# Handing over between two stages of a decoder step: the first gate weights and h loaded in the stage before, the sample's rows handed on in SBUF

## The chip, the cores and the metric

The kernel runs on one core of one Trainium2 chip, as one launch. The metric is the time of one execution on the device in microseconds (us), median of a few runs. fp32 throughout; matrix products are made exact enough by splitting each operand into a high and a low part (three products instead of one).

## The reference, cut to what matters

One layer of a decoder on a prompt of 2048 rows and on 32 sample rows (8 sequences x 4 positions), D_MODEL 1024:

```python
h = rms_norm(x, norm1_g) * (1 + scale1) + shift1
u, v_a, q, k, v_b, gates = jnp.split(h @ w_in, PROJ_SPLITS, axis=-1)
out_a = chunk_spatial_gate(gelu(u), layer_norm(gelu(v_a)), w_s, b_s)      # mixer A, 512 wide
out_b = attention(rope(q), rope(k), v_b)                                   # mixer B, 512 wide
g_a, g_b = split(sigmoid(gates))
merged = g_a * (out_a @ w_pa) + g_b * (out_b @ w_pb)
x = x + gate1 * (merged @ w_o)
# then: adaLN norm, top-2 of 32 experts, second residual, final norm
```

The sample rows go through the same weights; their attention also reads a cache of 128 keys and values for each of the 8 sequences.

## The kernel before, in words

The program has two Blocks, one behind the other. In a Block each of the five engines has its own list of instructions; engines meet only at semaphores, and at the end of a Block all five meet at a barrier, GpSimd clears the semaphores of the stage, and they meet again (`tools`, lines 111 to 128).

**The first Block, `sweep_mixers`**, goes over 16 tiles of 128 prompt rows and, as a 17th tile (index S), the 32 sample rows. It has the weights of both mixers in SBUF (`w_mix_hi`, `w_mix_lo`), computes h of a tile, turns it and stores its high and low parts as `hT_split` in DRAM; the results of mixers A and B go, turned and split, to `oT_split`. For the sample tile, ScalarE rounds a high part (L450, L507, L579), VectorE makes the low part (L594, L658, L814), and SyncE stores them (L315, L328, L381). The last steps of the Block are the sample's attention over the cache: TensorE L991 and L992, VectorE L810, ScalarE L579, VectorE L814, SyncE L381. SyncE then waits until every store has landed.

**The second Block, `finish`**, starts with `gate_a`: for each of 17 tiles, h times the gate columns of `w_in` (8 slices of 128 rows), out_a times `w_pa` (4 slices), out_b times `w_pb` (4 slices). SyncE loads the 16 slices (L1066, L1079; 512 KB each) into `w_gate_raw` and `w_out_raw`, and between them the sample's h and results (L1042, L1047, forms of 32 columns) and those of the first prompt tile. ScalarE rounds slice k (L1125), VectorE makes its low part in place of the raw one (L1160) once TensorE has used the raw slice for the sample rows (L1248). VectorE adds the sample's high and low parts up again into `sample_T` (L1164, L1169). In `first_tiles` TensorE takes the sample rows one slice ahead of the first prompt tile: sample(0), sample(1), slice 0, sample(2), slice 1 and so on. Then come two products with `w_ada` (L1281) and tiles 2 to 16 in a loop, each of which waits for its loads. Order on SyncE is the order in the code: the 16 slices, `w_ada` twice, then the loads of tile 2.

The same raw places are filled a second time by `gate_b`. Up to here slices k and k+8 share a semaphore (`raw_in[k % 8]`).

Of the kernel before, what the change touches and what calls it, by code (L numbers as in the profile page):

```python
# [92 lines left out]
def program(nc, a, outs):  # L93
    stack = ExitStack()
    with stack:
# [18 lines left out]
        }  # L114
        sweep_mixers(nc, a, s, kept, outs)
# [41 lines left out]
def sweep_mixers(nc, a, s, kept, outs):  # L157
# [3 lines left out]
    with ExitStack() as ctx:  # L161
        sb, sem = tools(nc, ctx)
        ps = banks(nc, ctx, "mix")
        with nc.sbuf_tensor("w_mix_raw", [P, KD, MIX_COLS], F32) as w_raw:
            pass
# [5 lines left out]
        wa = (w_hi, w_lo)  # L171
        x = sb("x_rows", [P, D])
        hT = [sb(f"hT_{n}", [P, KD, P], F32R) for n in ("hi", "lo")]
        mod = sb("mod_prompt", [P, 2, D])
        mod_s = sb("mod_sample", [MS, 2, D])
# [12 lines left out]
        obT_f = sb("out_b_T_sample", [P, 4, MS])[:, :, :]  # L188
# [17 lines left out]
        sq = sb("squares", [P, D])  # L206
# [20 lines left out]
        smp_turned, smp_scored, smp_dve, smp_max, smp_out = [sem(f"sample_{n}") for n in ("turned", "pe", "dve", "max", "out")]  # L227
# [32 lines left out]
        def _(sp):  # L260
# [61 lines left out]
            def rows_a(i, m):  # L322
                sp.wait_ge(oaT_lo, i + 1)
                dst = s["oT"][bass.ds(i, 1), 0, :, :] if not isinstance(i, int) else s["oT"][i:i + 1, 0, :, :]
                if m == P:
                    sp.dma_start(dst.rearrange("o p c -> p (o c)"), oaT[:, :, :].rearrange("p n c -> p (n c)").bitcast(F32)).then_inc(stored_oa, 16)
                else:
                    sp.dma_start(dst.rearrange("o p (c m) -> p (o c) m", m=P)[:, :, 0:m],  # L328
                                 oaT[:, :, :].rearrange("p n (k m) -> p (n k) m", m=P)[:, :, 0:m].bitcast(F32)).then_inc(stored_oa, 16)
# [16 lines left out]
            rows_a(0, P)  # L346
            with sp.Fori(1, NT - 2) as i:
                angles(i + 1, P)
                rows_b(i - 1)
                ahead(i + 2)  # L350
                stores(i + 1, P)
                rows_a(i, P)
# [7 lines left out]
            rows_a(NT - 2, P)  # L360
# [6 lines left out]
            stores(S, MS)  # L367
            rows_a(NT - 1, P)
# [69 lines left out]
        def _(act):  # L438
# [63 lines left out]
            def out_a(i, m, first):  # L502
# [3 lines left out]
                view = lambda t: t.rearrange("p (k m) -> p k m", m=P)[:, :, 0:m]  # L506
                nc.scalar.copy(view(oaT[:, 0, :]), view(ps[2][:, :])).then_inc(oaT_hi, 1)  # L507
# [8 lines left out]
            def tile(i, first=False, m_next=P):  # L516
# [15 lines left out]
                out_a(i, P, first)  # L532
# [38 lines left out]
            out_a(S, MS, False)  # L571
# [5 lines left out]
            act.wait_ge(smp_out, 1)  # L577
            act.wait_ge(stored_ob, 16 * NT)
            nc.scalar.copy(obT[:, 0, :].rearrange("p (k m) -> p k m", m=P)[:, :, 0:MS], obT_f).then_inc(obT_hi, 1)  # L579

        @block.vector
        def _(dve):
# [72 lines left out]
            def low_a(i, m):  # L655
                dve.wait_ge(oaT_hi, i + 1)
                view = lambda t: t.rearrange("p (k m) -> p k m", m=P)[:, :, 0:m]
                nc.vector.tensor_tensor(view(oaT[:, 1, :]), view(ps[2][:, :]), view(oaT[:, 0, :]).bitcast(F32),  # L658
                                        ALU.subtract).then_inc(oaT_lo, 1)
# [46 lines left out]
            def tile(i, mask_i, first=False, m_next=P, g_next=mod):  # L706
# [12 lines left out]
                low_a(i, P)  # L719
# [52 lines left out]
            low_b(NT - 1)  # L772

# [10 lines left out]
            low_a(S, MS)  # L784
# [23 lines left out]
            for g in range(NKV):  # L808
                src = ps[6][g * HD:(g + 1) * HD, 0:DEC_B * HQ].rearrange("p (b g c t) -> p g c b t", b=DEC_B, g=NKV, c=NC)[:, g]
# [191 lines left out]
def gate_a(nc, a, s, kept, sem, ps, weights, shared):  # L1001

    with ExitStack() as ctx:
# [5 lines left out]
        hb = sb("h_parts", [P, 2, 2 * D], F32R)  # L1009
# [10 lines left out]
        sample_h, sample_o, summed = sem("ga_sample_h"), sem("ga_sample_o"), sem("ga_sample_summed")  # L1020
        first_h, tile_in = sem("ga_first_h"), (sem("ga_tile_in0"), sem("ga_tile_in1"))
# [9 lines left out]
        landed = lambda k: 16 * (k // 8 + 1) + (16 if k >= KD + 4 else 0)  # L1031

        def slices():
            for k in range(KD):
                yield a["w_in"][0, k * P:(k + 1) * P, GATE_A:GATE_A + D]
            for k in range(4):
                yield a["w_pa"][0, k * P:(k + 1) * P, :]

        def on_sync(sp):
            def load_h(tile, par, m, done=None):  # L1040
# [1457 lines left out]
```

## Time and profile before

| | |
|---|---|
| time, median of 3 runs | 2024.82 us (2024.26 to 2030.19) |
| the profiled execution | 2026.46 us |
| its span, first to last instruction | 2024.8 us |
| TensorE busy in the span | 1896.6 us (94%) |
| TensorE's granted clock, mean | 0.960 of 2.4 GHz |
| DMA, mean | 188 GB/s |

In the rows below, TensorE appears twice: PE is the matmul, PEld the load of its stationary operand, which overlaps. DVE is VectorE, ACT ScalarE, POOL GpSimd; SPq is SyncE's queue, which issues DMAs. A name before `<-` is written, the names behind it are read; `L1248` is a line of the kernel. A bracket at the end of a row says how long the engine had been idle and what ended that. Times on the left are microseconds from the span's start, and where busy time is given it is not yet the time that the chain needs: matmuls are pipelined and overlap one another.

### The profile page before, as it was taken

The page shows a single profiled execution, that of the slowest core. Times are in us where ns is not written, and L with a number is a line of the kernel's source. Part 1 is how long each engine was busy: PE and PEld are TensorE (multiplying, and loading weights), DVE is VectorE, ACT ScalarE, POOL GpSimd, SP SyncE. Part 2 cuts the span into 40 slices and gives each one's busy share as a digit, 9 for nine tenths or more (in the row PEclk, how much of TensorE's full clock was granted, in tenths as well). Part 3 has the DMA queues.
Part 4 walks back from the last instruction along what each step waited for, and adds up shares of the span by engine and source line. Part 5 has one row for each costly group of instructions (what it writes and reads, how often), then busy time and mean ns, then how long its engine had stood idle before and what let it go on. Part 6 is the DMA issues. An engine that isn't in the chain of part 4 may idle for free.

```text
span 2024.8 us, 29311 instructions
## 1 busy us (share of the span) xinstructions
PE 1896.6 (94%) x9169; PEld 1427.9 (71%) x9170; DVE 1082.2 (53%) x1901; ACT 752.1 (37%) x1318; POOL 328.6 (16%) x337
## 2 busy tenths in 40 slices
PE   6999999999699999998999999992999999999966
PEld 2778877877367777776888888872667777776622
DVE  4777777777330000014455555555666666666647
ACT  3445554444221001013111111112566666666612
POOL 0111101110000000001011111101233333333411
PEclk7999999999699999999999999995999999999978
DMA  9212222122485554448444444437497464889686
GB/s 376 108 75 86 106 105 97 74 96 95 130 302 181 197 201 166 170 153 325 157 145 145 145 145 145 145 132 264 152 349 273 141 213 142 314 286 364 218 317 283
DMA packets 184473, 380.60 MB, mean 188 GB/s; under 512 B 41116, under 2 KB 112972, under 8 KB 177232
## 3 DMA queue, kind: packets, MB, share of 16 engines
q1 hardware_dynamic: 145824, 319.10, 44.1%
q0 software_dynamic: 20848, 52.32, 6.8%
q10 hardware_dynamic: 17760, 8.67, 1.5%
q8 instruction: 22, 0.36, 0.1%
q14 instruction: 19, 0.16, 0.0%
HBM read 295.16 MB, written 104.26 MB: 197 GB/s over the span
## 4 chain that ended last, share of the span: by engine, by line
PE 63%; DMA 4%; DVE 3%; issue 1%; SPq 1%; ACT 1%; ACTq 0%; POOL 0%; DVEq 0%; POOLq 0%
PE fin L152 16%; PE fin L154 15%; PE fin L153 15%; PE fin L2353 9%; PE fin L2322 2%; PE fin L1771 2%; PE fin L1807 1%; DMA w_gate_raw<-in_w_in 1%; DMA mixer_parts<-oT_split 1%; PE fin L1281 1%; DVE expert_gate_up L2298 1%; PE fin L2393 1%; DVE expert_gate_up L2302 1%; DMA w_out_raw<-in_w_o 1%; DVE expert_down L2291 1%
## 5 line engine op out<-in xcount | busy, mean ns | idle before, releaser
L2250 DVE TENSOR_TENSOR gate_up_lo<-expert_gate_up,gate_up_hi 128x2048 fp32r<-128x2048 f32 x102 | 233.6, 2292 | 149.0 <-ACT gate_up_hi L2155 145.6
L2155 ACT CAST gate_up_hi<-expert_gate_up 128x2048 fp32r x102 | 194.6, 1909 | 87.5 <-issue 87.5
L152 PE MATMUL mix<-w_mix_hi,hT_hi 128*128 128x512 f32 (+3 forms) x544 | 203.1, 373 | 3.8 <-DVE hT_lo L594 2.5
L153 PE MATMUL mix<-w_mix_hi,hT_lo 128*128 128x512 f32 (+3 forms) x544 | 198.7, 365 | 0.0
L154 PE MATMUL mix<-w_mix_lo,hT_hi 128*128 128x512 f32 (+3 forms) x544 | 198.2, 364 | 0.0
L2353 PE MATMUL fin<-expert_down,hidden_T 128*128 x400 | 182.6, 600 | 4.8 <-ACT hidden_T L2163 4.2
L1189 DVE SCALAR_TENSOR_TENSOR ma_rows<-tanh_rows,fin 128x512 f32<-128x512 f32 x32 | 20.6, 684 | 311.3 <-PE fin L154 160.9
L152 PE MATMUL fin<-gate_up_hi,gathered_T_hi 128*128 128x512 f32 x400 | 161.7, 404 | 4.2 <-DVE gathered_T_lo L2241 4.2
L154 PE MATMUL fin<-gate_up_lo,gathered_T_hi 128*128 128x512 f32 x400 | 158.1, 395 | 0.0
L153 PE MATMUL fin<-gate_up_hi,gathered_T_lo 128*128 128x512 f32 x400 | 157.6, 394 | 0.0
L2085 POOL DMA_INDIRECT gathered<-h_rows,row_tokens x52 | 130.0, 2501 | 43.8 <-PE fin L2322 17.9
L2353 PEld LDWEIGHTS fin<-expert_down,hidden_T 128*128 128x128 f32 x400 | 73.0, 193 | 78.5 <-issue 78.5
L152 PEld LDWEIGHTS mix<-w_mix_hi,hT_hi 128*128 128x128 f32 (+1 forms) x544 | 100.6, 185 | 37.2 <-issue 20.3
L154 PEld LDWEIGHTS mix<-w_mix_lo,hT_hi 128*128 128x128 f32 (+1 forms) x544 | 100.5, 185 | 19.1
L2091 POOL DMA_INDIRECT weighted_rows<-y_block,row_records x50 | 63.4, 1268 | 302.7 <-ACT y_block L2171 290.8
L153 PEld LDWEIGHTS mix<-w_mix_hi,hT_lo 128*128 128x128 f32 (+1 forms) x544 | 100.7, 185 | 16.2
L152 PE MATMUL fin<-w_gate_hi,h_parts_b 128*128 128x512 f32 x256 | 102.6, 401 | 6.0 <-issue 4.8
L152 PE MATMUL fin<-w_out_hi,merged_T_hi 128*128 128x512 f32 x256 | 102.3, 400 | 2.5 <-issue 2.5
L152 PE MATMUL fin<-w_gate_hi,h_parts 128*128 128x512 f32 x256 | 102.8, 402 | 1.0 <-DMA mixer_parts<-oT_split 1.0
L153 PE MATMUL fin<-w_out_hi,merged_T_lo 128*128 128x512 f32 x256 | 100.8, 394 | 0.0
L154 PE MATMUL fin<-w_out_lo,merged_T_hi 128*128 128x512 f32 x256 | 100.6, 393 | 0.0
L152 PE MATMUL fin<-w_out_hi,mixer_parts 128*128 128x512 f32 x256 | 100.5, 393 | 0.0
(343 smaller groups left out, 3769.1 us busy)
## 6 DMA issues: line engine op xcount, KB each, us to landing
expert_gate_up<-in_w_gate SPq DMA_DIRECT2D x32, 1024.0 KB
expert_gate_up<-in_w_up SPq DMA_DIRECT2D x32, 1024.0 KB
expert_down<-in_w_down SPq DMA_DIRECT2D x32, 1024.0 KB
h_parts<-hT_split SPq DMA_DIRECT2D x16, 1024.0 KB, 5.2
mixer_parts<-oT_split SPq DMA_DIRECT2D x32, 512.0 KB, 8.2
w_ada_part<-in_w_ada SPq DMA_DIRECT2D x16, 1024.0 KB, 10.6
h_parts_b<-hT_split SPq DMA_DIRECT2D x16, 1024.0 KB, 4.8
expert_down<-weighted_rows SPq DMA_DIRECT2D x12, 1024.0 KB, 7.9
```

Source lines behind the costliest of these rows:

```text
L152: nc_mm(out, left[0], right[0], start=first, stop=False)
L153: nc_mm(out, left[1], right[0], start=False, stop=False)
L154: return nc_mm(out, left[0], right[1], start=False, stop=last)
L1189: last = nc.vector.scalar_tensor_tensor(out=ma[:, par, at], in0=tg[:, at], scalar=1.0, in1=ps[2 + n][:, :], op0=ALU.add, op1=ALU.mult)
L1281: done = nc.tensor.matmul(ps[6 + half][32 * j:32 * j + R, :], c_now[half][:, :], wc[half][:, j, :], start=first, stop=last, tile_position= ...
L1771: last = nc.tensor.transpose(ps[bank + k // 4][:, (k % 4) * P:(k % 4 + 1) * P], src[:, k * P:(k + 1) * P], ident[:, :])
L2085: pool.indirect_dma_start(out=xg[:, slot % 2, :], out_offset=None, in_=s["h2"], in_offset=bass.IndirectOffsetOnAxis(ap=idx[:, slot, 0:1].b ...
L2091: pool.indirect_dma_start(out=s["y2"], out_offset=bass.IndirectOffsetOnAxis(ap=rec[:, slot, 0:1].bitcast(U32), axis=0), in_=y[:, half(slot ...
L2155: nc.scalar.copy(wg[par][0][:, n * HG:(n + 1) * HG], ring[:, bass.ds(slot * GU + n * HG, HG)]).then_inc(w_hi, 1)
L2250: nc.vector.tensor_tensor(wg[par][1][:, at], ring[:, bass.ds(slot * GU + n * HG, HG)], wg[par][0][:, at].bitcast(F32), ALU.subtract).then_ ...
L2322: last = nc.tensor.transpose(ps[k // 4][:, (k % 4) * P:(k % 4 + 1) * P], xg[:, par, k * P:(k + 1) * P], ident[:, :])
L2353: last = nc.tensor.matmul(ps[5 + n][:, :], hT[par][:, k, :], downs[:, bass.ds(at, 512)], start=(k == 0), stop=(k == 1))
```

## The change: what it does

1. The places of the gate weights, of `sample_T` and of `h_parts` are laid out before the first Block (`gate_places`), over the mixers' weights and, for h, over `hT`; their load semaphores live for the whole program (`kept`), one for each of the 16 slices. The small lists of `finish` move out of their way, and so do x, the squares and two modulation rows of the mixers. As `kept` things now have semaphores of the program's own scope, one more clearing with its barriers stands at the end of the program.
2. At the end of its work in the mixers' Block, once TensorE has used the mixers' weights for the last time (`u_done` of tile S) and all prompt h is stored, SyncE issues all 16 weight slices and the h of the first prompt tile. It doesn't wait for them there.
3. The sample's h and results are no longer stored and loaded. VectorE adds h's two parts into `sample_T` directly, and copies out_a and out_b from PSUM into it.
4. `gate_a` thus starts with weights that are there or on their way; its SyncE list begins with the first tile's results.

```diff
@@ sweep_mixers, SyncE @@
             rows_b(NT - 2)
-            stores(S, MS)
-            rows_a(NT - 1, P)
+            rows_a(NT - 1)
             rows_b(NT - 1)
...
             sp.wait_ge(ln_ready, S + 1)
             sp.dma_start(chunk_v[0].rearrange("b t w -> (b t) w"), v[0:MS, :]).then_inc(stored_kv, 16)
-            rows_a(S, MS)
-            sp.wait_ge(obT_lo, S + 1)
-            sp.dma_start(s["oT"][S, 1].rearrange("p (c m) -> p c m", m=P)[:, :, 0:MS],
-                         obT[:, :, :].rearrange("p n (k m) -> p (n k) m", m=P)[:, :, 0:MS].bitcast(F32)).then_inc(stored_ob, 16)
+            sp.wait_ge(u_done, S + 1)
+            sp.wait_ge(stored_h, 32 * NT)
+            for k, src in enumerate(gate_slices(a)):
+                sp.dma_start(gate_raw(k), src).then_inc(kept["raw_in"][k], 16)
+                if k == 1:
+                    sp.wait_ge(smp_kept, 1)
+                    sp.dma_start(first_h[:, 1, :].bitcast(F32), s["hT"][0]).then_inc(kept["first_h"], 16)
+            for c in range(NC):
+                for g in range(NKV):
+                    k, h = KD + 4 + c, g * NC + c
+                    sp.dma_start(gate_raw(k)[g * HD:(g + 1) * HD], a["w_pb"][0, h * HD:(h + 1) * HD, :]).then_inc(kept["raw_in"][k], 16)
             sp.wait_ge(stored_kv, 80)
-            sp.wait_ge(stored_h, 32 * (NT + 1))
-            sp.wait_ge(stored_oa, 16 * (NT + 1))
-            sp.wait_ge(stored_ob, 16 * (NT + 1))
+            sp.wait_ge(stored_oa, 16 * NT)
+            sp.wait_ge(stored_ob, 16 * NT)
@@ ScalarE @@
             gelu_u(S, MS, False)
-            out_a(S, MS, False)
...
-            act.wait_ge(smp_out, 1)
-            act.wait_ge(stored_ob, 16 * NT)
-            nc.scalar.copy(obT[:, 0, :].rearrange("p (k m) -> p k m", m=P)[:, :, 0:MS], obT_f).then_inc(obT_hi, 1)
@@ VectorE @@
             low_b(NT - 1)
+            nc.vector.tensor_tensor(sample_T[:, 0:KD, :], hT[0][:, :, 0:MS].bitcast(F32), hT[1][:, :, 0:MS].bitcast(F32), ALU.add).then_inc(smp_kept, 1)
...
-            low_a(S, MS)
+            dve.wait_ge(oa_turned, S + 1)
+            nc.vector.tensor_copy(sample_T[:, KD:KD + 4, :], ps[2][:, :].rearrange("p (k m) -> p k m", m=P)[:, :, 0:MS]).then_inc(smp_kept, 1)
...
-                last = nc.vector.tensor_copy(obT_f[g * HD:(g + 1) * HD, :, :].rearrange("p c (b t) -> p c b t", t=DEC_T), src)
-            last.then_inc(smp_out, 1)
-            dve.wait_ge(obT_hi, S + 1)
-            view = lambda t: t.rearrange("p (k m) -> p k m", m=P)[:, :, 0:MS]
-            nc.vector.tensor_tensor(view(obT[:, 1, :]), obT_f, view(obT[:, 0, :]).bitcast(F32), ALU.subtract).then_inc(obT_lo, 1)
+                nc.vector.tensor_copy(sample_T[rows, KD + 4:, :].rearrange("p c (b t) -> p c b t", t=DEC_T), src).then_inc(smp_kept, 1)
@@ gate_a, SyncE @@
-            for k, src in enumerate(slices()):
-                if k >= 8:
-                    sp.wait_ge(raw_hi, k - 7)
-                sp.dma_start(raw(k), src).then_inc(raw_in[k % 8], 16)
-                if k == 0:
-                    load_h(NT, 0, MS, sample_h)
-                    load_h(0, 1, P, first_h)
-                if k == 4:
-                    load_o(NT, 0, MS, sample_o)
-                if k == KD:
-                    load_o(0, 1, P)
...
+            load_o(0, 1)
             load_ada(0, 0)
             load_ada(0, 1)
             load(2, 0)
@@ gate_a, VectorE @@
-            dve.wait_ge(sample_h, 16)
-            nc.vector.tensor_tensor(sample_T[:, 0:KD, :], parts[:, 0:KD, :], parts[:, KD:, :], ALU.add).then_inc(summed, 1)
...
+            low(range(KD + 4))
@@ gate_a, TensorE, sample(k) @@
-                if k in (0, KD):
-                    pe.wait_ge(summed, 3 if k else 1)
-                pe.wait_ge(raw_in[k % 8], landed(k))
+                pe.wait_ge(raw_in[k], landed(k))
```

How SyncE's list changes around the border of the two Blocks. Before, from the store of the sample's v to the last load of tile 2 (the two branches are the border):

```order
L378 DMA out<-v_rows 32x512
L328 DMA oT_split<-out_a_T 1024x1x32
L381 DMA oT_split<-out_b_T 1024x1x32
L161 UNCONDITIONAL_BRANCH
L2443 UNCONDITIONAL_BRANCH
L1066 DMA w_gate_raw<-in_w_in 128x1024
L1042 DMA h_parts<-hT_split 128x16x32
L1042 DMA h_parts<-hT_split 128x2048
L1066 DMA w_gate_raw<-in_w_in 128x1024 x4
L1047 DMA mixer_parts<-oT_split 128x8x32 x2
L1066 DMA w_gate_raw<-in_w_in 128x1024 x3
L1066 DMA w_out_raw<-in_w_pa 128x1024
```

and the same stretch now, up to the results of tile 2:

```order
L383 DMA out<-v_rows 32x512
L387 DMA w_gate_raw<-in_w_in 128x1024 x2
L390 DMA h_parts<-hT_split 128x2048
L387 DMA w_gate_raw<-in_w_in 128x1024 x6
L387 DMA w_out_raw<-in_w_pa 128x1024 x4
L394 DMA w_out_raw<-in_w_pb 64x1024 x8
L168 UNCONDITIONAL_BRANCH
L2435 UNCONDITIONAL_BRANCH
L1044 DMA mixer_parts<-oT_split 128x1024 x2
L1056 DMA w_ada_part<-in_w_ada 128x4x512 x2
L1039 DMA h_parts<-hT_split 128x2048
L1044 DMA mixer_parts<-oT_split 128x1024 x2
```

Twenty weight loads and one of h stand ahead of the border instead of behind it, and the four small sample transfers in each direction are gone. VectorE's list at the end of the first Block, before:

```order
L805 COPY probs_T<-mix 128x256
L806 COPY probs_T<-mix 4x256
L810 COPY out_b_T_sample<-mix 64x128 x2
L814 TENSOR_TENSOR out_b_T<-out_b_T_sample,out_b_T 128x4x32
L161 UNCONDITIONAL_BRANCH
L2461 UNCONDITIONAL_BRANCH
L1164 TENSOR_TENSOR sample_T<-h_parts 128x256
L1160 TENSOR_TENSOR w_gate_lo<-w_gate_raw,w_gate_hi 128x1024 x4
```

and now:

```order
L811 COPY probs_T<-mix 128x256
L812 COPY probs_T<-mix 4x256
L817 COPY sample_T<-mix 64x128 x2
L168 UNCONDITIONAL_BRANCH
L2453 UNCONDITIONAL_BRANCH
L1139 TENSOR_TENSOR w_gate_lo<-w_gate_raw,w_gate_hi 128x1024 x8
```

The copy from PSUM is the last step of the Block now, and the first low part the first step of the next.

## Rows read from the trace of the kernel before

**Rows 1.** The page: busy time, share of the span and instructions of TensorE.

```profile
PE 1896.6 (94%) x9169; PEld 1427.9 (71%) x9170; DVE 1082.2 (53%) x1901; ACT 752.1 (37%) x1318; POOL 328.6 (16%) x337
```

**Rows 2.** Waits, 505 to 600 us: who waited for whom, total us, times, longest.

```profile
PE fin L1248 <- DVE sample_T L1164: 10.8, 1, 10.8
...
DVE sample_T L1164 <- DMA h_parts<-hT_split: 9.1, 1, 9.1
...
PE fin L1248 <- DMA w_gate_raw<-in_w_in: 3.2, 1, 3.2
```

**Rows 3.** Windows: stretch, its length, busy us by engine, granted clock, DMA share, GB/s.

```profile
524.00:533.60 9.60, 9.09 (x32) 7.99 (x32) 0.42 (x3) 0.00 (x0) 0.00 (x0) 0.50 0.00 0
...
549.60:553.40 3.80, 3.80 (x18) 2.03 (x14) 1.23 (x1) 3.14 (x3) 0.00 (x0) 0.50 1.13 308
553.40:584.80 31.40, 31.40 (x201) 17.83 (x199) 19.38 (x21) 13.21 (x15) 1.41 (x2) 1.00 1.02 357
...
587.70:610.70 23.00, 22.99 (x105) 18.10 (x105) 1.37 (x3) 1.92 (x4) 0.53 (x1) 1.00 0.61 228
```

**Rows 4.** Timeline, 533.4 to 540 us, all engines: start, us, engine, line, operation.

```profile
533.56 0.59 DVE L810 COPY out_b_T_sample<-mix 64x128 f32<-64x128 f32 x2 [9.18 <-PE mix L992]
...
534.52 0.29 DVE L814 TENSOR_TENSOR out_b_T<-out_b_T_sample,out_b_T 128x128 fp32r<-128x128 f32 x1 [0.36 <-ACT out_b_T L579]
534.84 0.55 SPq L381 DMA_DIRECT2D oT_split<-out_b_T  x1
538.84 0.37 SPq L1066 DMA_DIRECT2D w_gate_raw<-in_w_in  x1
```

**Rows 5.** Lines 161, 127, 128 (barriers, clearing): ns min/median/max, first and last start.

```profile
L161 SPq DRAIN x1: 13/13/13, 537.5 to 537.5; - x1
...
L127 POOLq EVENT_SEMAPHORE_RANGE_CLEAR  x2: 568/676/783, 538.0 to 2023.8; - x2
...
L128 SPq DRAIN  x2: 7/7/7, 537.8 to 2023.5; - x2
...
L128 SPq EVENT_SEMAPHORE  x2: 17/17/17, 538.8 to 2024.8; - x2
```

**Rows 6.** Timeline of TensorE, 533 to 588 us.

```profile
544.37 1.08 PE L1248 MATMUL fin<-w_gate_raw,sample_T 128*32 128x256 f32 x8 [10.85 <-DVE sample_T L1164]
...
549.62 0.80 PE L152 MATMUL fin<-w_gate_hi,h_parts 128*128 128x512 f32 x1
...
553.49 0.54 PE L152 MATMUL fin<-w_gate_hi,h_parts 128*128 128x512 f32 x1
...
584.78 1.91 PE L1281 MATMUL fin<-w_ada_part,c_now 128*9 128x512 f32 x16
587.71 0.49 PE L152 MATMUL fin<-w_gate_hi,h_parts 128*128 128x512 f32 x1 [1.02 <-DMA mixer_parts<-oT_split]
```

**Rows 7.** Timeline of SyncE's queue, which issues DMAs: three stretches.

```profile
2.07 3.68 SPq L266 DMA_DIRECT2D w_ada_slices<-in_w_ada  x7
...
9.06 13.65 SPq L275 DMA_DIRECT2D w_mix_raw<-in_w_in  x8
...
516.69 0.32 SPq L378 DMA_DIRECT2D out<-v_rows  x1
...
556.03 4.99 SPq L1079 DMA_DIRECT2D w_out_raw<-in_w_pb  x8
```

**Rows 8.** Groups of ScalarE and VectorE, 538 to 588 us: busy us, mean ns.

```profile
L1160 DVE TENSOR_TENSOR w_gate_lo<-w_gate_raw,w_gate_hi 128x1024 fp32r<-128x1024 f32 x8 | 9.8, 1226 | 11.3 <-PE fin L1248 10.3 <-ACT w_out_hi L1125 0.9
...
L1125 ACT CAST w_gate_hi<-w_gate_raw 128x1024 fp32r<-128x1024 f32 x8 | 8.4, 1050 | 16.0 <-DMA w_gate_raw<-in_w_in 16.0
```

**Rows 9.** Timeline of VectorE, 512 to 522 us.

```profile
515.19 1.29 DVE L782 COPY x_rows<-mix 128x512 f32<-128x512 f32 x2 [1.62 <-PE mix L821]
```

**Rows 10.** DMA queues, 516 to 520, then 538.8 to 587.7 us: packets, MB, share.

```profile
q8 instruction: 1, 0.02, 1.5%
...
q8 instruction: 2, 0.03, 0.2%
```

More of the change, by code:

```diff
@@ L114, in program @@
         }
+        sb, sem = tools(nc, stack)
+        kept["small"] = sb("small", [P, 48])
+        kept["half"] = sb("minus_half_row", [P, 1])
+        kept["rms"] = sb("rms_c", [P, 4, 4])
+        kept["lists"] = list_tables(sb)
+        kept["raw_in"], kept["first_h"] = [sem(f"g_raw_in{n}") for n in range(2 * KD)], sem("ga_first_h")
+        kept["gates"] = gate_places(nc)
         sweep_mixers(nc, a, s, kept, outs)
@@ L163, in sweep_mixers @@
         ps = banks(nc, ctx, "mix")
+        raws, _, sample_T, first_h = kept["gates"]
+        gate_raw = lambda k: raws[k // KD][:, k % KD, :]
         with nc.sbuf_tensor("w_mix_raw", [P, KD, MIX_COLS], F32) as w_raw:
@@ L500, in gelu_u, with out_a @@
                 nc.scalar.activation(u[0:m, :], ps[2][0:m, :], ACT.Gelu_apprx_tanh).then_inc(u_gelu, 1)
-            def out_a(i, m, first):
+            def out_a(i, first):
                 act.wait_ge(oa_turned, i + 1)
@@ L531, in tile @@
                 high(i + 1, m_next)
-                out_a(i, P, first)
+                out_a(i, first)
                 softmax(i)
@@ L1123, in high @@
                 for k in ks:
-                    act.wait_ge(raw_in[k % 8], landed(k))
+                    act.wait_ge(raw_in[k], landed(k))
                     nc.scalar.copy(w(0, k), raw(k)).then_inc(raw_hi, 1)
@@ L1160, in low @@
                     nc.vector.tensor_tensor(w(1, k), raw(k), w(0, k).bitcast(F32), ALU.subtract).then_inc(raw_lo, 1)
-            dve.wait_ge(sample_h, 16)
-            parts = view(hb[:, 0, :].bitcast(F32), MS, 16)
-            nc.vector.tensor_tensor(sample_T[:, 0:KD, :], parts[:, 0:KD, :], parts[:, KD:, :], ALU.add).then_inc(summed, 1)
-            low(range(4))
-            dve.wait_ge(sample_o, 32)
-            for n in range(2):
-                parts = view(ob[:, 0, n, :].bitcast(F32), MS, 8)
-                nc.vector.tensor_tensor(sample_T[:, KD + 4 * n:KD + 4 * n + 4, :], parts[:, 0:4, :], parts[:, 4:, :], ALU.add).then_inc(summed, 1)
-            low(range(4, KD + 4))
+            low(range(KD + 4))
             dve.wait_ge(tanhed, 1)
@@ L1742, in sample @@
             def sample(bank, lhs, k0, k, done):
-                pe.wait_ge(raw_in[(k0 + k) % 8], landed(k0 + k))
+                pe.wait_ge(raw_in[k0 + k], landed(k0 + k))
                 for j in range(4):
@@ L1869, in load_down, with list_tables @@
     sp.dma_start(ww, a["w_down"][0, bass.ds(e, 1), :, :].rearrange("o (k p) d -> p (o k) d", p=P)).then_inc(done, 16)
[L1872 removed]
+def list_tables(sb):
     ni = sb("blocks_i", [P, NE], I32)
@@ L1882, in list_blocks, with gate_places, gate_slices @@
     rest = sb("pairs_after_first", [1, 1], I32)
+    return ni, n, zero, ends, ends_i, m, f, lists, rest
+def gate_places(nc):
+    with ExitStack() as ctx:
+        split, raws = [], []
+        for m in ("gate", "out"):
+            with nc.sbuf_tensor(f"w_{m}_raw", [P, KD, D], F32) as w_raw:
+                raws.append(w_raw)
+            lo, hi = [ctx.enter_context(nc.sbuf_tensor(f"w_{m}_{n}", [P, KD, D], F32R)) for n in ("lo", "hi")]
+            split.append((hi, lo))
+        sample_T = ctx.enter_context(nc.sbuf_tensor("sample_T", [P, 2 * KD, MS], F32))
+        h_parts = ctx.enter_context(nc.sbuf_tensor("h_parts", [P, 2, 2 * D], F32R))
+        return raws, split, sample_T, h_parts
+def gate_slices(a):
+    for k in range(KD):
+        yield a["w_in"][0, k * P:(k + 1) * P, GATE_A:GATE_A + D]
+    for k in range(4):
+        yield a["w_pa"][0, k * P:(k + 1) * P, :]
+def list_blocks(nc, kept, sem, ps, small, ready):
+    ni, n, zero, ends, ends_i, m, f, lists, rest = kept["lists"]
     step_done, listed, moved = sem("l_step"), sem("l_listed"), sem("l_moved")
```

102 lines of the change are left out of this document (39 added, 63 removed).

## The prediction

> **What bounds the kernel now.** I read the busy shares first. TensorE is busy for 94% of the span [rows 1], so the place to look is where it is not. The waits of the stretch around the border of the two Blocks come next: TensorE stands 10.8 us until the sample's h is in SBUF, whose addition had itself waited 9.1 us for the DMA that brings it back from DRAM, then 3.2 us for the second weight slice [rows 2], and 1.02 us for the results of tile 2 [rows 6]. The windows show what follows: from 553.40 to 584.80 TensorE is busy for all of 31.40 us at clock 1.00, and tile 2, 587.70 to 610.70, takes 23.00 us of which 22.99 are busy [rows 3]. So once `gate_a` is under way it is bound by TensorE, and what is saved ahead of its first slice should pass to the end.
>
> **The hand-over (parts 2 and 3 of the change).** Before, the Block's last steps are: copy L810, 533.56 to 534.15; ScalarE L579; VectorE L814 to 534.81; store L381, issued at 534.84; the first DMA of the next Block at 538.84 [rows 4]. SyncE reaches the barrier at 537.5, when that store has landed, and goes on at 538.8 after the clearing [rows 5]. So barrier, clearing and barrier take 1.3 us, and the DMA follows at once. Now the copy is the last step, since SyncE waits only for stores issued by 516.69 and earlier [rows 7]. The Block's work ends at 534.15, the next begins at 534.15 + 1.3 = 535.5, that is 3.3 us earlier.
>
> **The additions on VectorE.** The sum of h's parts into `sample_T` is one instruction more, priced like the removed L1164, some 0.4 us. VectorE has 1.62 us of idle time ahead of L782 right behind it [rows 9], so it costs nothing; if that cover were missing, it would cost 0.4. The copy of out_a replaces L658 and ScalarE's part goes: nothing on the path either, since the chain behind it goes over TensorE's scores.
>
> **SyncE's 21 issues ahead of the border.** They start at 516.69 + 0.32, about 517.1 (`u_done` and the prompt stores are older). Seven loads of 1 MB are issued in 3.68 us, 0.53 each, and eight of `w_pb` in 4.99, 0.62 each, part of it waiting [rows 7]. 13 x 0.53 + 8 x 0.62 = 11.9, so SyncE is through by 529, 5 us before VectorE. Could its queue fill up, so that it holds the Block? In the trace it does at 9.06, where eight loads of 0.9 MB take 13.65 us [rows 7], but by then over 8 MB had been issued in 7 us. Here 9.4 MB in all are issued over 12 us; at 357 GB/s, the rate of the busy stretch [rows 3], 4 MB of it have landed by then, so 5 MB are in flight. I take no delay; the upper end is in a rival below.
>
> **The first slice.** Slice 0 and 1 and h were issued first and have landed by the border (2 MB at 357 GB/s is 6 us, hence by 525). What stands ahead of TensorE's slice 0 is then the high part, 1.05 us, and the low part, 1.23 us [rows 8], each with about 0.1 us of signalling. The sample groups sample(0) and sample(1) run beside them, 1.08 us each at the low clock [rows 6]. 535.5 + 0.1 + 1.05 + 0.1 + 1.23 + 0.1 = 538.1. Before, slice 0 starts at 549.62 [rows 6]. **Term 1: 549.62 - 538.1 = 11.5 us earlier.** Behind it ScalarE (1.05 per slice) and VectorE (1.23) are faster than TensorE, which takes (584.78 - 553.49) / 15 = 2.1 per slice [rows 6], so neither becomes the bound.
>
> **The clock.** The granted clock is 0.50 already while TensorE works on the small products of the sample's attention, 524.00 to 533.60, stays there over the idle time, and is still 0.50 for 549.60 to 553.40, when slice 0 runs; it is 1.00 from 553.40 [rows 3]. That is 1.2 and then 2.4 GHz. TensorE's dense work began only 1 us before slice 0. Now two sample groups, 2.1 us, run nearly straight into slice 0, so between 0 and 2.1 us of the slow stretch fall on them instead, and each such microsecond is worth half. A value in the middle: **term 2: 0.5 us gained** (0 to 1.05). The bound below nothing: if the short gap between sample(1) and slice 0 delays the rise by as long as the slow stretch before, 3.8 us, it costs 1.9.
>
> **The loads of tile 2.** Before, all transfers from 538.84 up to tile 2's amount to 14.7 MB, and TensorE waits 1.02 us for the last of them [rows 6]. Now 9.4 MB start at 517.1 and are in by 543.5 at 357 GB/s; 5.2 MB more (tile 1's results, two of `w_ada`, tile 2) are queued from 535.5 and are in by 558. TensorE gets to tile 2 at 538.1 + (584.78 - 549.62) - 0.5 + 1.9 = 574.7, so 16 us later than needed. **Term 3: 1.0 us gained.**
>
> **The clearing at the program's end.** Another clearing and barrier: the one at the end of the span goes from 2023.5 to 2024.8, of which the clearing is 0.57 to 0.78 us; that at the border goes from 537.8 to 538.8 [rows 5]. **Term 4: 1.2 us lost** (0 to 1.3).
>
> **The other layout.** New addresses and sixteen load semaphores instead of eight change no duration that the trace shows; later stages stand as they were. Nothing, either way.
>
> **Sum.** 11.5 + 0.5 + 1.0 - 1.2 = 11.8 us. The profiled execution took 2026.46 us, 1.64 above the median of the runs shown; I take the gain off each alike: 2014.7 for an execution like it, 2013.0 for the median. With the bounds of the terms, 11.5 + 1.05 + 1.0 - 0 = 13.6 and 11.5 - 1.9 + 1.0 - 1.3 = 9.3, this case alone gives 2011.2 to 2015.5.
>
> **Rival 1: the engines get going later than SyncE.** That engines start 0.1 us behind the barrier is seen only of SyncE [rows 4, 5]. The others waited for data there: the first high part starts 3.9 us behind the barrier. A start-up of up to 3.9 us was hidden and would show now: gain 7.9, time 2016.9. For it: nothing in the trace excludes it. Against: a fetch of instructions lies at 516 to 520, ahead of the border [rows 10], so that the code behind it may be at hand.
>
> **Rival 2: the barrier waits for the loads, or the transfers bind.** SyncE drains at the border for 13 ns [rows 5], but with all DMAs landed; no row shows a drain with loads in flight. Did it wait, the Block would end at 543.5, slice 0 start at 543.5 + 1.3 + 2.6 = 547.4: gain 2.2 + 0.5 + 1.0 - 1.2 = 2.5, time 2022.3. A full queue that holds SyncE gives something between this and the forecast. Against: the list of waits ahead of the border has no load in it.
>
> **Rival 3, slower: the loads hold up the tail of the first Block.** The mixers' tail fetches code at 516 to 520 [rows 10], just when 9.4 MB are put on the same 16 DMA engines. If that fetch is served behind them it comes at 543.5, and an engine that needs it stands: the remaining 16 us of the tail (518 to 534) then end at 559.5, slice 0 starts at 559.5 + 1.3 + 2.6 = 563.4, 13.8 us later than before: 2024.82 + 13.8 - 1.5 + 1.2 = 2038.3. It makes the change a loss once the fetch is delayed by more than about 12 us. Against it: two such fetches fall into 538.8 to 587.7 [rows 10], where the DMA engines are full, and TensorE is busy there for 31.40 of 31.40 us once it has begun [rows 3].
> The Trainium skill ("DMA: Bandwidth & Descriptors", section "Queues, rings and completion order") says that a DMA engine goes round its queues packet by packet, by which a fetch is delayed by a packet, not by 9 MB, and this rival would cost nothing; the full stretch above agrees. The same page, under "Back-pressure in remote DMA", says that writes stalled at a full SBUF port stall that engine's other queues too; it speaks of transfers between cores, and no row here shows such a stall. By it some of this rival's price would be due.
>
> **How the numbers follow.** What a measurement can tell from no change is about 0.3%, 6.1 us: faster is below 2018.7, slower above 2030.9. The forecast has 0.74, rival 1 0.12, rival 2 0.07, rival 3 0.04, others 0.03. Faster: the forecast and rival 1 and a part of the rest, 0.87; the same: rival 2, 0.08; slower 0.05. The time is the forecast's, 2013.0. The range takes the forecast's bounds with the scatter of a median, 2009.5 below, and rival 1 above with some of what lies between it and rival 2: 2018.5.
>
> **What would show it.** Right: the first DMA of the second Block near 535.5; slice 0 near 538; TensorE with no wait for a DMA from there to tile 2, which starts near 575 instead of 587.71; the span's end 12 us earlier with a second clearing of about 1.2 us in it. SyncE's 21 issues over by 529. Term 2 shows in the length of the stretch at clock 0.50 behind 538. Wrong: a first high part much later than the first DMA (rival 1), a border near 544 (rival 2), TensorE's attention products later than 524.4 (rival 3), or waits for transfers that come back in the loop of tiles.

## The result, and the profile after

| | before | changed |
|---|---|---|
| median of 4 runs | 2025.74 us (2024.26 to 2030.19) | 2013.88 us (2013.14 to 2014.41) |
| ratio | | 0.9939, 95% interval 0.9927 to 0.9952 |
| span of the profiled execution | 2024.8 us | 2012.8 us |

The changed kernel is about 12 us faster, 0.6%; by the interval the gain lies between 9.7 and 14.8 us. Forecast were 2013.0 us for the median and a gain of 11.8. Two runs lay far above all others of their kernel (10828 us in e3_late_first_h, 6324 us in g2_lead_again) and are left out of the medians and ratios below.

SyncE's queue in the changed kernel (start, us, queue, line, what it issues), from the first early load to the loads of tile 2; it answers to [rows 7] and to the last two of [rows 4]:

```profile
517.15 0.86 SPq L387 DMA_DIRECT2D w_gate_raw<-in_w_in  x2
518.06 0.43 SPq L390 DMA_DIRECT2D h_parts<-hT_split  x1
518.53 3.14 SPq L387 DMA_DIRECT2D w_gate_raw<-in_w_in  x6
521.71 2.59 SPq L387 DMA_DIRECT2D w_out_raw<-in_w_pa  x4
524.35 6.63 SPq L394 DMA_DIRECT2D w_out_raw<-in_w_pb  x8
535.69 0.81 SPq L1044 DMA_DIRECT2D mixer_parts<-oT_split  x2
...
539.73 6.85 SPq L1039 DMA_DIRECT2D h_parts<-hT_split  x1
```

The early loads start at 517.15 as computed, and SyncE is through with them at 530.98, 3 us before VectorE ends the Block. The first DMA of the second Block is at 535.69 instead of 538.84. Later one issue is slow: the load of tile 2's h takes 6.85 us instead of some 0.4, as it would with a full queue, at a time when nobody needs SyncE.

The engines at the border, from the timelines of VectorE, ScalarE and TensorE; to be read beside [rows 4], [rows 9] and [rows 6]:

```profile
513.26 0.41 DVE L777 TENSOR_TENSOR sample_T<-hT_hi,hT_lo 128x256 f32<-128x256 f32 x1
...
515.34 1.29 DVE L787 COPY x_rows<-mix 128x512 f32<-128x512 f32 x2 [1.28 <-PE mix L824]
...
533.71 0.61 DVE L817 COPY sample_T<-mix 64x128 f32<-64x128 f32 x2 [9.18 <-PE mix L995]
```

```profile
535.69 7.67 ACT L1104 CAST w_gate_hi<-w_gate_raw 128x1024 fp32r<-128x1024 f32 x8 [13.97 <-PEq L135]
```

```profile
535.72 1.93 PE L1217 MATMUL fin<-w_gate_raw,sample_T 128*32 128x256 f32 x16 [2.04 <-PEq L135]
538.21 0.79 PE L159 MATMUL fin<-w_gate_hi,h_parts 128*128 128x512 f32 x1 [0.56 <-DVE w_gate_lo L1139]
...
574.32 1.91 PE L1250 MATMUL fin<-w_ada_part,c_now 128*9 128x512 f32 x16
576.16 0.50 PE L159 MATMUL fin<-w_gate_hi,h_parts 128*128 128x512 f32 x1
```

ScalarE makes all eight high parts in a row, 7.67 us without a wait for a DMA. TensorE starts 0.05 us behind the release of the barrier, slice 0 comes at 538.21 (before 549.62), and tile 2 at 576.16 (before 587.71) with no bracket: its data lay ready.

The windows of the same stretch (stretch, length, busy us of PE, PEld, DVE, ACT, POOL, granted clock, DMA share, GB/s) answer to [rows 3]:

```profile
524.00:533.60 9.60, 9.01 (x32) 7.98 (x32) 0.54 (x2) 0.00 (x0) 0.00 (x0) 0.50 1.02 417
535.70:538.20 2.50, 1.93 (x16) 0.67 (x16) 1.26 (x2) 2.50 (x3) 0.00 (x0) 0.50 1.08 326
538.20:544.00 5.80, 5.79 (x19) 3.55 (x20) 2.32 (x2) 5.80 (x7) 0.00 (x0) 0.50 1.02 242
544.00:574.30 30.30, 30.30 (x191) 17.01 (x189) 17.73 (x18) 8.68 (x12) 1.41 (x2) 1.00 0.53 194
576.10:599.10 23.00, 23.00 (x108) 18.07 (x104) 1.37 (x3) 1.86 (x4) 1.07 (x2) 1.00 0.66 240
```

The DMA engines are now full during the sample's attention, where they were idle, and TensorE's 32 products last there as long as before. The clock is at 0.50 (1.2 GHz of 2.4) for 5.8 us of slices instead of 3.8.

One thing in these windows is easily missed. The DMA share is 1.02 both in 524.00 to 533.60 and in 538.20 to 544.00, but 417 GB/s arrive in the first and 242 in the second. By their place in the queue the later transfers are the eight loads of `w_pb`, of 64 rows each; the kernel before has the same fall with full engines, from 420 GB/s (556 to 561 us) to 238 (565 to 570). Why these are slower wasn't tested. It matters for whatever is queued behind them, as e2_loads_only and e3_late_first_h show.

Barriers and clearing (lines 168, 134, 135 now; ns min/median/max, first and last start), and VectorE's last operation; they answer to [rows 5]:

```profile
L168 SPq DRAIN  x1: 153/153/153, 531.3 to 531.3; - x1
...
L134 POOLq EVENT_SEMAPHORE_RANGE_CLEAR  x3: 131/568/718, 534.8 to 2012.3; - x3
...
L135 SPq EVENT_SEMAPHORE  x3: 17/17/17, 535.6 to 2012.7; - x3
```

```profile
2002.28 1.27 DVE L2299 SCALAR_TENSOR_TENSOR late_x<-late_x,rms_c,expert_gate_up 32x1024 f32<-32x1024 f32 x1 [0.97 <-POOL rms_c L2118]
```

SyncE's drain takes 0.15 us with the loads in flight. The third clearing is the short one, 0.13 us. From the start of VectorE's last operation to the end of the span it is now 10.5 us (2002.28 to 2012.8; 10.4 in both other profiles of the changed kernel). In the kernel before the row of that operation is this one, and the span ends at 2024.8, 9.95 us behind its start:

```profile
2014.85 1.27 DVE L2302 SCALAR_TENSOR_TENSOR late_x<-late_x,rms_c,expert_gate_up 32x1024 f32<-32x1024 f32 x1 [0.97 <-POOL rms_c L2121]
```

### The profile page after: what moved, and what is told of

Read it like the earlier page. It is cut to its first block, busy times and chain, and to the rows that moved or that the text cites. A ratio compares the mean times of both kernels' runs of the same rounds, so it can differ in the third digit from the quotient of the medians.

```text
span 2012.8 us, 29307 instructions
## 1 busy us (share of the span) xinstructions
PE 1896.9 (94%) x9169; PEld 1427.4 (71%) x9170; DVE 1081.2 (54%) x1898; ACT 749.5 (37%) x1316; POOL 329.4 (16%) x337
## 4 chain that ended last, share of the span: by engine, by line
PE 65%; DMA 3%; DVE 2%; SPq 1%; issue 1%; ACT 1%; ACTq 0%; POOL 0%; DVEq 0%; POOLq 0%
PE fin L159 16%; PE fin L160 16%; PE fin L161 16%; PE fin L2350 9%; PE fin L2319 2%; PE fin L1740 1%; PE fin L1776 1%; PE fin L2390 1%; PE fin L1250 1%; DMA expert_down<-weighted_rows 1%; DMA w_out_raw<-in_w_o 1%; DMA w_gate_raw<-in_w_in 1%; PE fin L2338 1%; DVE expert_gate_up L2295 0%; PE fin L1217 0%
## 5 line engine op out<-in xcount | busy, mean ns | idle before, releaser
L159 PE MATMUL fin<-w_gate_hi,h_parts_b 128*128 128x512 f32 x256 | 102.9, 402 | 5.8 <-issue 4.8
L159 PE MATMUL fin<-w_gate_hi,h_parts 128*128 128x512 f32 x256 | 103.3, 404 | 0.6 <-DVE w_gate_lo L1139 0.6
L160 PE MATMUL fin<-w_gate_hi,h_parts_b 128*128 128x512 f32 x256 | 100.8, 394 | 0.0
L161 PE MATMUL fin<-w_gate_lo,h_parts_b 128*128 128x512 f32 x256 | 100.7, 394 | 0.0
L160 PE MATMUL fin<-w_gate_hi,h_parts 128*128 128x512 f32 x256 | 100.7, 393 | 0.0
## 6 DMA issues: line engine op xcount, KB each, us to landing
expert_gate_up<-in_w_up SPq DMA_DIRECT2D x32, 1024.0 KB, 10.9
```

What stands on the lines that cost most here:

```text
L159: nc_mm(out, left[0], right[0], start=first, stop=False)
L160: nc_mm(out, left[1], right[0], start=False, stop=False)
L161: return nc_mm(out, left[0], right[1], start=False, stop=last)
```

## The experiments

Ratios are to the kernel before, each from runs on the same chip, with 95% intervals; the changed kernel itself, measured twice more, gave 0.9938 (0.9924 to 0.9951) and 0.9934 (0.9921 to 0.9947).

### One half of the change alone

**e1_handover_only**: the loads go behind the border again.

```diff
             sp.wait_ge(stored_h, 32 * NT)
-            (the 21 early loads)
...
+            for k, src in enumerate(gate_slices(a)):       # gate_a, SyncE
+                sp.dma_start(raw(k), src).then_inc(raw_in[k], 16)
+                if k == 0:
+                    sp.dma_start(hb[:, 1, :].bitcast(F32), s["hT"][0]).then_inc(first_h, 16)
+                if k == KD:
+                    load_o(0, 1)
```

> The sample's rows and results are handed on in SBUF, as in the changed kernel, but all 16 weight slices and the first h are issued only in the second Block. Theory (the two halves of the gain are separate: 3.1 us from the shorter end of the first Block, the rest from loads that lie ahead of the border): the first DMA of the second Block starts near 535.7, slice 1 has landed some 7.5 us later, slice 0 starts near 543.5, tile 2 near 581 without a wait for a DMA, time about 2019.5. Rival (the loads of the sample's parts, in pieces of 128 bytes, were no part of the delay): slice 0 starts 10.8 us behind the first DMA as before, near 546.5, time about 2022.5. Rival (the loads ahead of the border bring nothing by themselves): 2014.

Measured: 2019.6 us, ratio 0.9970 (0.9957 to 0.9983). In its trace, SyncE and TensorE:

```profile
536.65 0.36 SPq L1050 DMA_DIRECT2D w_gate_raw<-in_w_in  x1
```

```profile
540.50 1.08 PE L1217 MATMUL fin<-w_gate_raw,sample_T 128*32 128x256 f32 x8 [5.86 <-DMA w_gate_raw<-in_w_in]
544.26 1.08 PE L1217 MATMUL fin<-w_gate_raw,sample_T 128*32 128x256 f32 x8 [2.69 <-DMA w_gate_raw<-in_w_in]
545.28 0.80 PE L159 MATMUL fin<-w_gate_hi,h_parts 128*128 128x512 f32 x1
```

Slice 0 starts 8.6 us behind the first DMA: 10.8 before, 2.5 in the changed kernel. So the hand-over in SBUF brings some 6 us alone, of which the sample's small loads (three in the kernel before, not four as the list of changes has it), no longer between the weights, are 2.2. The time is as expected; slice 0 is 1.8 us later than expected: the first DMA came 1.0 us later in this profile, and sample(1), 1.08 us long, still runs between the landing of the second slice and slice 0.

**e2_loads_only**: the early loads stay, the sample goes over DRAM as before. The store of out_a stands ahead of the early loads, which therefore start at 520.39 and not at 517.15. The sample's last store, and the loads that bring it back:

```diff
                     sp.dma_start(gate_raw(k)[g * HD:(g + 1) * HD], ...)      # last of the early loads
+            sp.wait_ge(obT_lo, S + 1)
+            sp.dma_start(s["oT"][S, 1]..., obT...).then_inc(stored_ob, 16)
...
+            sp.dma_start(view(hb[:, 0, :], MS, 16).bitcast(F32), view(s["hT"][NT], MS, 16)).then_inc(sample_h, 16)
             load_o(0, 1)
```

> The weight slices and the first h are issued ahead of the border, as in the changed kernel, but the sample's h and results go over DRAM as before. Theory (the loads need the hand-over in SBUF, since the last store of the Block stands in SyncE's queue behind 9.4 MB of loads): that store is issued near 534.9 but lands only when the loads are through, near 543; the first DMA of the second Block starts near 544.5, the sample's h is in SBUF near 549, slice 0 starts near 550; time about 2026, no gain over the kernel before. Rival (the store is not held up): border as before, first DMA at 538.8, the sample's h 3 to 5 us later, slice 0 near 545; time about 2020.

Measured: 2033.4 us, ratio 1.0037 (1.0025 to 1.0049): 7.5 us slower than the kernel before. SyncE's waits, then its queue, then TensorE's first slice, then two windows (the last two numbers are DMA share and GB/s):

```profile
SPq L405 <- DMA oT_split<-out_b_T: 14.6, 1, 14.6
```

```profile
535.58 0.59 SPq L401 DMA_DIRECT2D oT_split<-out_b_T  x1
552.28 0.60 SPq L1080 DMA_DIRECT2D h_parts<-hT_split  x1
```

```profile
558.75 0.79 PE L159 MATMUL fin<-w_gate_hi,h_parts 128*128 128x512 f32 x1 [0.57 <-DVE w_gate_lo L1164]
```

```profile
540.00:545.00 5.00, 0.00 (x0) 0.00 (x0) 0.00 (x0) 0.00 (x0) 0.00 (x0) 0.50 1.05 265
545.00:550.70 5.70, 0.00 (x0) 0.00 (x0) 0.00 (x0) 0.00 (x0) 0.00 (x0) 0.50 0.86 190
```

A store that took 2.4 us takes 15 when it is issued behind 9.4 MB of loads, and the whole barrier waits for it. The theory's direction holds, its size does not: I had expected no gain, and it is a loss. The store was to land near 543 and lands at 550.7, for two reasons: the loads ahead of it start 3.2 us later than I had assumed, and the last of them, with the store, move at 265 and 190 GB/s and not at 357. The rival, a store that isn't held up, is out.

**e3_late_first_h**: one load of the 21, the first tile's h, behind the border.

```diff
                 sp.dma_start(gate_raw(k), src).then_inc(kept["raw_in"][k], 16)
-                if k == 1:
-                    sp.wait_ge(smp_kept, 1)
-                    sp.dma_start(first_h[:, 1, :].bitcast(F32), s["hT"][0]).then_inc(kept["first_h"], 16)
...
+            sp.dma_start(hb[:, 1, :].bitcast(F32), s["hT"][0]).then_inc(first_h, 16)     # gate_a
             load_o(0, 1)
```

> The changed kernel with one load moved: the h of the first prompt tile is issued as the first DMA of the second Block instead of the third of the early loads. Theory (that load is on the path, and 2.6 MB of weights are still queued ahead of it): it lands 9 to 11 us behind 535.7, slice 0 starts near 546 instead of 538.2, time about 2021.5. Rival (small beside the weights): it lands in the 5.2 us of an undisturbed load, slice 0 near 541, time 2016.5.

Measured: 2022.80 us, ratio 0.9988 (0.9978 to 0.9998). TensorE:

```profile
548.50 1.08 PE L1215 MATMUL fin<-w_gate_raw,sample_T 128*32 128x256 f32 x8 [11.27 <-DMA h_parts<-hT_split]
549.51 0.80 PE L159 MATMUL fin<-w_gate_hi,h_parts 128*128 128x512 f32 x1
```

All weights of the first slices are there, and TensorE waits 11.27 us for one load of 1 MB that stands behind the rest. It costs 10 of the 12 us. TensorE goes on 12.4 us behind the issue at 536.12; the theory had 9 to 11. Too little was left in the queue to explain this at 357 GB/s: 6.8 MB had moved by 536.1, so some 1.6 MB of weights stood ahead of this load. But from there to 544 the full DMA engines moved only 243 to 251 GB/s, the rate seen above for the loads of `w_pb`. Whether the loads issued behind it shared the engines too wasn't tested.

### The clock: waits of TensorE filled

**e4_lookahead2**: two sample groups ahead, so that sample(2) fills the 0.56 us ahead of slice 0.

```diff
-                    if k + 1 < KW:
-                        sample(k + 1)
+                    for n in (1, 2) if k == 0 else (k + 2,):
+                        if n < KW:
+                            sample(n)
```

> The changed kernel, but TensorE takes the sample rows two slices ahead of the first prompt tile instead of one, so that sample(2) fills its 0.56 us of idle time between sample(1) and slice 0. Theory (that gap delays the rise of the granted clock from 0.50 to 1.00, which now comes 5.8 us behind the start of slice 0 instead of 3.8 before): the rise comes about 3.4 us earlier, near 540.6, and the first product ends 1.7 us earlier; time about 2012.2. Rival (the rise doesn't depend on the gap): the clock rises 8.3 us behind TensorE's restart, as in the changed kernel, slice 0 starts 0.5 us later but one sample group is done; time 2013.9, no change.

Measured: 2011.18 us, ratio 0.9928 (0.9916 to 0.9940). It was repeated later beside the changed kernel as **g2_lead_again**, with the changed kernel as **g3_after_third**:

> The two-slice lead alone once more, beside the one before and the changed kernel on the same chip. Theory (a real gain of 1 to 2 us over the changed kernel): ratio 0.9928 to 0.9932. Rival (the first measurement was scatter): 0.9939.

> The changed kernel as the yardstick of this group. Both theories: ratio about 0.9938.

Measured: 2010.55 us, ratio 0.9928 (0.9915 to 0.9941), against 2012.73 us and 0.9934 (0.9921 to 0.9947) for g3_after_third. TensorE in e4_lookahead2:

```profile
536.53 2.79 PE L1217 MATMUL fin<-w_gate_raw,sample_T 128*32 128x256 f32 x24 [2.04 <-PEq L135]
539.25 0.80 PE L159 MATMUL fin<-w_gate_hi,h_parts 128*128 128x512 f32 x1
...
573.04 1.90 PE L1251 MATMUL fin<-w_ada_part,c_now 128*9 128x512 f32 x16
```

and in **f1_after_again**, the changed kernel as yardstick of the next group:

> The changed kernel once more, as the yardstick of this group. Both theories: about 0.994 of the kernel before; slice 0 near 538.2 and the rise of the clock between 5.5 and 8.5 us behind TensorE's restart.

```profile
536.71 1.94 PE L1217 MATMUL fin<-w_gate_raw,sample_T 128*32 128x256 f32 x16 [2.04 <-PEq L135]
539.21 0.80 PE L159 MATMUL fin<-w_gate_hi,h_parts 128*128 128x512 f32 x1 [0.56 <-DVE w_gate_lo L1139]
...
574.12 1.91 PE L1250 MATMUL fin<-w_ada_part,c_now 128*9 128x512 f32 x16
```

f1_after_again took 2014.24 us. From TensorE's restart to the `w_ada` products the three profiles of the changed kernel took 38.6 us (535.72 to 574.32), 37.4 and 37.4, the two with the longer lead 36.5 and 36.0. The profiles of the next section agree: 38.2 and 37.3 without the longer lead (f2_warm_gaps, f3_warm_all), 35.5 and 35.2 with it (g1_gaps_and_lead, f4_warm_best). The work is the same, so the difference is the clock and the filled gap. The gap's 0.56 us alone doesn't make 1.5 us on average, the clock does the rest.

The theory's size fails, though: it had the clock rise near 540.6, and in e4_lookahead2 it rises at about 542.2, 5.7 us behind the restart. In f1_after_again and g3_after_third, which have the gap, it is 5.9, in the first profile of the changed kernel 8.3, in g2_lead_again 4.6 (each worked out from the granted clock of a window over the rise). One kernel's own profiles differ by more than e4_lookahead2 and f1_after_again do. So it isn't shown that the gap delays the rise. What the traces do show is that the stretch is shorter in all four profiles with the longer lead than in all five without it. By time the ratios point the same way each time, but their intervals overlap: likely, not shown by time alone.

**f2_warm_gaps**: TensorE works in its two waits of the sample's attention.

```diff
+            def keep_busy(n):
+                for _ in range(n):
+                    nc.tensor.matmul(ps[7][:, 0:256], ident[:, :], ln[:, 0, 0:256], start=True, stop=True)
...
             last.then_inc(smp_scored, 1)
+            keep_busy(6)
             pe.wait_ge(smp_dve, 13)
...
             last.then_inc(smp_scored, 1)
+            keep_busy(2)
             pe.wait_ge(smp_dve, 15)
```

> The changed kernel, with TensorE kept busy in its two waits of the sample's attention: six products of the identity with 256 columns while the softmax runs (3.6 us idle), two while the probabilities are copied (0.8 us), into a PSUM bank that nobody reads. Theory (the granted clock falls to 0.50 because TensorE stands still there, and it is this that makes the sixteen pairs of small products last 9.1 us): the clock stays 1.00 into the products, which take 4.6 to 6 us; the first Block ends 3 to 4 us earlier; time about 2010. Rival (the small products, 32 columns wide, count as too little work to keep the clock, or their length does not hang on it): the clock falls during them all the same, the Block ends at the same time or up to 1 us later; time 2013.5 to 2015.

Measured: 2010.62 us, ratio 0.9932 (0.9918 to 0.9945), beside 0.9938 of f1_after_again, whose runs go from 2007.92 to 2016.48: by time no difference is shown. TensorE, then the window of the small products:

```profile
518.79 4.54 PE L977 MATMUL mix<-ln_rows,identity 128*128 128x256 f32 x12
523.17 0.60 PE L824 MATMUL mix<-identity,scores 128*128 128x128 f32 x4
523.61 1.03 PE L977 MATMUL mix<-ln_rows,identity 128*128 128x256 f32 x4
524.60 0.41 PE L1000 MATMUL mix<-probs_T,mod_prompt 128*128 128x32 f32 x2
...
532.48 1.94 PE L1223 MATMUL fin<-w_gate_raw,sample_T 128*32 128x256 f32 x16 [2.31 <-PEq L135]
```

```profile
524.60:530.20 5.60, 5.57 (x33) 4.82 (x32) 0.00 (x0) 0.00 (x0) 0.00 (x0) 0.96 1.03 418
```

The small products of the attention (L1000 and the line behind it, 16 pairs) now take 5.6 us at a granted clock of 0.96, not 9.1 at 0.50: their length does hang on the clock. The second Block starts near 532.4, 3.3 us earlier. But the clock falls again behind the attention, and the slices are as slow as before (534.98 to the `w_ada` products at 570.63, 35.7 us). The first six added products themselves fell into a stretch at the lower clock and took 4.54 us.

**f3_warm_all**: three more such products among the small ones. **f4_warm_best**: besides, four behind the attention, and the lead of two slices.

```diff
                 last = nc.tensor.matmul(ps[6][:, at], v_new[:, b, :], pT2_s[:, at], start=False, stop=True)
+                if b % 2 == 1 and b < DEC_B - 1:
+                    keep_busy(1)
             last.then_inc(smp_scored, 1)
+            keep_busy(4)                      # f4_warm_best only
```

> As the one before, with one more product of 256 columns behind every second sequence of the sample's attention (three in all, 0.43 us each at clock 1.00). Theory (the clock falls during the small products unless wide ones are among them): the clock is 1.00 over the whole attention and still when the second Block starts, so slice 0 and 1 are fast too; time about 2007. Rival (the length of the small products does not hang on the clock, which only the slices feel): the attention lasts 9.1 us and 1.3 us more; the slices at the start gain 2 to 3 us; time 2012.5.

> As the one before, with four more products of 256 columns behind the attention (1.7 us at clock 1.00, beside VectorE's copy and the barrier) and the sample rows taken two slices ahead of the first tile. Theory (each wait of TensorE around the border is filled, so the clock stays 1.00 from the mixers to the gates): slice 0 starts about 2.7 us behind the second Block's first DMA and all slices take 2.1 us; time about 2005.5. Rival (the clock falls for other reasons, and the added products lie on the path, since the barrier waits for TensorE): time 2011 to 2014, no better than the two-slice lead alone.

Measured: f3_warm_all 2013.09 us, 0.9939 (0.9926 to 0.9953); f4_warm_best 2013.22 us, 0.9942 (0.9929 to 0.9956). Neither is better than the changed kernel. TensorE in f4_warm_best:

```profile
519.81 2.86 PE L977 MATMUL mix<-ln_rows,identity 128*128 128x256 f32 x12
...
534.01 3.78 PE L977 MATMUL mix<-ln_rows,identity 128*128 128x256 f32 x8
539.16 2.79 PE L1226 MATMUL fin<-w_gate_raw,sample_T 128*32 128x256 f32 x24 [1.37 <-PEq L135]
```

The clock fell in spite of the three wide products (at about 528.1 here, 529.3 in f3_warm_all), and the four at the end then took 3.78 us, not 1.7, on the path to the barrier. The theory of both falls. The rival of f4_warm_best holds. That of f3_warm_all has the time nearly right (2012.5), but not for its reason: it took the length of the small products to be independent of the clock, and they are short up to 529.3, while the clock is 1.00.

**g1_gaps_and_lead**: the edits of f2_warm_gaps and e4_lookahead2 together.

> The changed kernel with two of the small edits together: TensorE kept busy in its two waits of the sample's attention, and the sample rows taken two slices ahead of the first tile. Theory (they act at two places, the first shortens the attention from 9.1 to 5.4 us, the second lets the clock rise earlier in the first slices): slice 0 starts about 3 us earlier than in the changed kernel and the slow stretch behind it is shorter; ratio about 0.9918 of the kernel before, 2009. Rival (what the first gives is spent again behind the border, since the clock then falls later and rises later): ratio about 0.993, like each alone.

Measured: 2009.39 us, ratio 0.9915 (0.9902 to 0.9928). TensorE:

```profile
519.11 2.86 PE L977 MATMUL mix<-ln_rows,identity 128*128 128x256 f32 x12
...
533.62 2.79 PE L1223 MATMUL fin<-w_gate_raw,sample_T 128*32 128x256 f32 x24 [2.04 <-PEq L135]
536.33 0.80 PE L159 MATMUL fin<-w_gate_hi,h_parts 128*128 128x512 f32 x1
```

```profile
526.60:531.50 4.90, 4.90 (x19) 4.32 (x18) 0.00 (x0) 0.00 (x0) 0.00 (x0) 0.52 1.02 415
```

This is the fastest version, 16 us below the kernel before, as the theory had it. Its first part gives less than expected: here the clock falls at about 526.6, in the middle of the small products, which take 7.3 us (524.24 to 531.57) and not the 5.6 of f2_warm_gaps. The six added products ran at clock 1.00 here (2.86 us, not 4.54), with 0.78 us of idle time behind them. Why the clock then falls sooner is open. The `w_ada` products of this version start at 569.10, against 574.12 in f1_after_again and 573.85 in g3_after_third. Beside the changed kernel of its own group (0.9934) the intervals still overlap by a little, but each of its five runs (2007.65 to 2011.07 us) is below each of the five of g3_after_third (2012.01 to 2013.07).

## Why the prediction was right, step by step

The path was the one forecast, and term 1, which carries the result, has the right size. Terms 2 and 4 were mis-sized, in opposite directions.

- **The border.** Forecast 535.5, measured 535.69 (TensorE 535.72). SyncE waits for nothing that is still under way. e2_loads_only shows what this rests on: with one store left behind the loads, the border comes at 552.28.
- **Additions on VectorE.** L777 takes 0.41 us at 513.26; the idle time ahead of the next copy shrinks from 1.62 to 1.28 us, and that copy starts where it did relative to its neighbours. No cost.
- **SyncE's issues.** Through at 530.98, forecast 529; the eight of `w_pb` took 0.83 each instead of 0.62. No cost, but the margin was 3 us, not 5.
- **Term 1, slice 0.** Forecast 538.1 and 11.5 us, measured 538.21 and 11.4. By e1_handover_only against the changed kernel, some 6 us of the whole are the hand-over and some 6.5 the early loads; by e2_loads_only and e3_late_first_h neither the loads without the hand-over, nor the weights without h, are worth anything like it.
- **Term 2, the clock: mis-sized.** Forecast 0.5 us gained. From slice 0 to the `w_ada` products it is 36.1 us in the changed kernel's first profile and 35.2 before (549.62 to 584.78): 0.95 lost. In the two other profiles it is 34.9, 0.25 gained. So the middle value was a guess within a scatter of 1.2 us between profiles of one kernel. Whether the gap of 0.56 us, which I had left to the lower bound, makes any of it is open: with the longer lead the same stretch takes 33.8 and 33.3 us, but it then holds one sample group less (about 1 us), and 33.8 is no gain against 34.9.
- **Term 3, tile 2.** The wait of 1.02 us is gone. All early and following loads were in by about 560, forecast 558, and needed at 576.
- **Term 4, the clearing.** Forecast 1.2 us lost, measured 0.55: the added clearing takes 0.13 us, not 0.57 to 0.78. I had priced it at clearings with many more semaphores; that the number of semaphores is the reason wasn't tested.
- **Sum.** 11.4 - 0.95 + 1.0 - 0.55 = 10.9 us of the span's 12.0. The remaining 1.1 us lie between tile 2 and VectorE's last operation: 1427.1 us before (587.71 to 2014.85), 1426.1 now (576.16 to 2002.28). It is no effect of the change that these traces can show: the same stretch takes 1428.4 us in f1_after_again and 1424.1 in g3_after_third, the same kernel. So two mis-sized terms and this rest cancel. That the total came out within 0.1 us of the forecast, with an interval of 2.5 us on either side, is luck; that it is about 12 is not.
- **Rival 1** (engines start late): out; ScalarE and TensorE start at 535.69 and 535.72. **Rival 2** (the barrier waits for loads): out; the drain takes 0.15 us with the loads in flight, and the slow issue came only at 539.73. **Rival 3** (the tail is held up): out; the attention products start at 524.59 against 524.44 before, with every step ahead of them shifted alike, at a DMA share of 1.02. The fetch of instructions itself is recorded later: between 521.5 and 522.0 instead of 519.0 and 519.5, and in all three profiles of the changed kernel some 3 us ahead of the attention products. It is 5 us ahead of them in the kernel before and in e1_handover_only, without the early loads. So the loads hold it up by some 2.5 us, not by the 24 of the rival, and this cost nothing on the path. Two rules of the Trainium skill were weighed there ("DMA: Bandwidth & Descriptors", sections "Queues, rings and completion order" and "Back-pressure in remote DMA"). The round of queues packet by packet agrees with a fetch that passes most of the loads; the stall by back-pressure was not seen in any run here.

## What to carry to other kernels

A barrier between two stages costs its own 1.3 us, but also everything that has to be fetched anew behind it: load the next stage's first operands before it, all of them, since one load left behind the rest cost 10 of 12 us. Whatever the barrier still waits for, stores above all, must be issued ahead of such loads or not exist at all; the same loads turned from a gain of 6 us into a loss of 7.5 when one small store stood behind them. Behind a stage with small products look at the granted clock, and fill TensorE's waits with work that is due anyway. By the traces, added products helped only where TensorE would have stood still, and cost where they lay on the path.

## What the runs showed of the hardware that was not expected

- A small store of 128 KB behind 9.4 MB of loads in the same queue took 15.1 us to land instead of 2.4; a load of 1 MB behind 8.4 MB of weights, 12.4 us from its issue to TensorE's next step.
- With the DMA engines full in both (share 1.02), 417 GB/s arrived in one stretch of the loads and 242 in another, so the share alone doesn't say how fast a queue empties.
- A fetch of instructions beside the early loads was recorded some 2.5 us later than without them; an all-engine barrier didn't wait for loads in flight (SyncE's drain took 0.15 us).
- Sixteen pairs of fp32 products of 32 columns took 9.1 us at a granted clock of 0.50 (1.2 GHz) and 5.6 us in f2_warm_gaps at 0.96, so they hang on the clock to a good part although each is so short. In the changed kernel TensorE was busy with them for 9.01 us of a stretch of 9.60, and the clock stayed at 0.50 throughout.
- The moment at which the clock rises behind a stage varies between profiles of the same kernel: 8.3 us behind TensorE's restart in one profile of the changed kernel, 5.9 in two others, with 1.2 us less for the same products.
